# Alternating wide and narrow matmuls in the gate and up products of eight feed-forward stages

## The reference

```
def rms_norm(x, g):
    return x * rsqrt(mean(x * x) + eps) * g

def swiglu_ffn(h, w_gate, w_up, w_down):          # 1024 -> 2816 -> 1024
    return (silu(h @ w_gate) * (h @ w_up)) @ w_down

x = x + 0.5 * swiglu_ffn(rms_norm(x, g), w_gate, w_up, w_down)     # eight of these
```

## Time and profile before

| | |
|---|---|
| median of 3 runs | 2270.24 us (2267.35 to 2273.36) |
| the profiled execution: its own time | 2273.36 us |
| its span, first to last instruction | 2271.6 us |
| mean granted TensorE clock | 0.980 |
| TensorE matmuls busy | 2154.5 us (95%) |
| weight loads busy | 1839.9 us (81%) |
| VectorE / ScalarE / GpSimd busy | 1529.0 / 1147.1 / 355.5 us |
| DMA | 375.61 MB, 165 GB/s on average |

### The profile page before, as it was taken

One profiled execution on the slowest core, in us unless ns is written; L12 is line 12 of the kernel. 1 busy time (PEld: TensorE's weight loads), 2 busy tenths in 40 slices (PEclk: granted clock), 3 DMA queues, 4 the chain that ended last, 5 costly groups with the idle time before them and its releaser, 6 DMA issues.

```text
span 2271.6 us, 40266 instructions
## 1 busy us (share of the span) xinstructions
PE 2154.5 (95%) x14196; PEld 1839.9 (81%) x14196; DVE 1529.0 (67%) x2387; ACT 1147.1 (50%) x1945; POOL 355.5 (16%) x474
## 2 busy tenths in 40 slices
PE   7999899999999899989999999997999998879997
PEld 6888678888888688878888988886888688858885
DVE  5667956676668766666666756666666794667665
ACT  5446655455547554555455554446544642235544
POOL 1111111112111011111110001111111012311110
PEclk9999999999999999999999999998999999989998
DMA  6555435555555245545565446554655330115552
GB/s 236 195 186 183 135 103 200 191 171 177 193 194 181 87 154 191 192 156 195 186 222 188 152 161 203 186 189 180 208 191 169 132 127 18 50 65 198 188 188 97
DMA packets 103827, 375.61 MB, mean 165 GB/s; under 512 B 11536, under 2 KB 11920, under 8 KB 103728
## 3 DMA queue, kind: packets, MB, share of 16 engines
q1 hardware_dynamic: 103728, 374.24, 48.8%
HBM read 373.15 MB, written 1.05 MB: 165 GB/s over the span
## 4 chain that ended last, share of the span: by engine, by line
PE 84%; DVE 9%; ACT 4%; issue 2%; POOL 1%; DMA 0%; SPq 0%; DVEq 0%; ACTq 0%; POOLq 0%
PE bank L795 27%; PE bank L799 14%; PE bank L186 12%; PE bank L187 12%; PE bank L188 12%; DVE w_lo L180 3%; PE bank L1929 2%; DVE work L1293 1%; ACT w_hi L173 1%; ACT act L410 1%; PE bank L356 1%; ACT work L399 1%; DVE act L508 0%; DVE work L1317 0%; PE bank L1939 0%
## 5 line engine op out<-in xcount | busy, mean ns | idle before, releaser
L795 PE MATMUL bank<-act,w_hi 128*128 128x512 f32 x2816 | 709.3, 394 | 5.3 <-DVE act L508 5.3
L795 PEld LDWEIGHTS bank<-act,w_hi 128*128 128x128 f32 x2816 | 519.8, 190 | 109.2 <-DVE w_lo L180 4.7
L712 DVE TENSOR_TENSOR w_lo<-raw,w_hi 128x1024 fp32r<-128x1024 f32 x432 | 502.8, 1219 | 2.5
L703 ACT ACTIVATE w_hi<-raw 128x1024 fp32r<-128x1024 f32 x432 | 425.0, 1050 | 2.4
L799 PEld LDWEIGHTS bank<-act,w_lo 128*128 128x128 f32 x2816 | 385.1, 191 | 27.8
L799 PE MATMUL bank<-act,w_lo 128*128 128x256 f32 x2816 | 393.3, 283 | 0.0
L180 DVE TENSOR_TENSOR w_lo<-raw,w_hi 128x1024 fp32r<-128x1024 f32 x248 | 295.2, 1220 | 96.5 <-ACT w_hi L173 96.1
L765 DVE TENSOR_TENSOR work<-bank,work 128x256 f32<-128x256 f32 x176 | 74.7, 424 | 387.4 <-ACT work L727 387.4
L742 POOL TENSOR_TENSOR work<-work,rb 128x256 f32<-128x256 f32 x176 | 129.7, 737 | 1053.5 <-DVE work L762 1053.5
L173 ACT ACTIVATE w_hi<-raw 128x1024 fp32r<-128x1024 f32 x248 | 251.6, 1051 | 58.0 <-PE bank L188 57.8
L186 PE MATMUL bank<-w_hi,g_hi 128*128 128x512 f32 x704 | 277.1, 394 | 0.9 <-DVE w_lo L180 0.3
(11 more groups left out here) (270 smaller groups left out, 2280.4 us busy)
## 6 DMA issues: line engine op xcount, KB each, us to landing
raw<-w_dram SPq DMA_DIRECT2D x680, 512.0 KB, 4.4
work<-rows_dram SPq DMA_DIRECT2D x13, 512.0 KB, 6.0
work<-rrows_dram SPq DMA_DIRECT2D x5, 512.0 KB, 3.2
x<-x_dram SPq DMA_DIRECT2D x2, 512.0 KB, 3.8
out<-x SPq DMA_DIRECT2D x4, 256.0 KB, 2.1
work<-g_dram SPq DMA_DIRECT2D x1, 640.0 KB, 9.0
const<-const_dram SPq DMA_DIRECT2D x1, 512.0 KB, 6.0
work<-dist_dram SPq DMA_DIRECT2D x2, 256.0 KB, 5.2
```

The lines of the kernel that those rows point to most:

```text
L703: nc.scalar.activation(c.w_hi[:, n % RING, :], c.raw[:, n % RING, :], ACT.Copy).then_inc(c.hi_ready, 1)
L712: nc.vector.tensor_tensor(c.w_lo[:, n % RING, :], c.raw[:, n % RING, :], c.w_hi[:, n % RING, :].bitcast(F32), ALU.subtract).then_inc(c.lo_ ...
L795: nc.tensor.matmul(bank[:, :], c.w_hi[:, slot(m), k * P:(k + 1) * P], c.act[:, k, :, :], start=k == 0, stop=False)
```

## The change

`by_high` and `by_low` become one function that issues the wide and the narrow matmul of one k. `hidden` alternates them: wide, narrow, wide, narrow, over the eight k. The start of a stage gives up its two halves: for each k it waits for the tile and issues wide and narrow of the gate unit, then wide and narrow of the up unit. The instructions, their operands and their number stay the same, as does the last matmul of each unit.

```diff
-    def by_high(m, bank, k):
-        nc.tensor.matmul(bank[:, :], c.w_hi[:, slot(m), k * P:(k + 1) * P], c.act[:, k, :, :], start=k == 0, stop=False)
-    def by_low(m, bank, k):
-        return nc.tensor.matmul(bank[:, 0:S], c.w_lo[:, slot(m), k * P:(k + 1) * P], c.act_hi[:, k, :],
-                                start=False, stop=k == KT - 1)
+    def hidden_tile(m, bank, k):
+        w = slice(k * P, (k + 1) * P)
+        nc.tensor.matmul(bank[:, :], c.w_hi[:, slot(m), w], c.act[:, k, :, :], start=k == 0, stop=False)
+        return nc.tensor.matmul(bank[:, 0:S], c.w_lo[:, slot(m), w], c.act_hi[:, k, :], start=False, stop=k == KT - 1)
 
     def hidden(pe, i, m, bank):
         unit_waited(pe, i, m)
         for k in range(KT):
-            by_high(m, bank, k)
-        for k in range(KT):
-            last = by_low(m, bank, k)
+            last = hidden_tile(m, bank, k)
         last.then_inc(c.unit_used, 1)
...
     def tensor(pe):
         unit_waited(pe, None, 0)
         unit_waited(pe, None, 1)
-        for half in (range(4), range(4, KT)):
-            for k in half:
-                join.tile_there(pe, k)
-                by_high(0, gate[0], k)
-                by_high(1, up[0], k)
-            for m, bank in ((0, gate[0]), (1, up[0])):
-                for k in half:
-                    last = by_low(m, bank, k)
-                if k == KT - 1:
-                    last.then_inc(c.unit_used, 1)
+        for k in range(KT):
+            join.tile_there(pe, k)
+            gate_last = hidden_tile(0, gate[0], k)
+            if k == KT - 1:
+                gate_last.then_inc(c.unit_used, 1)
+            up_last = hidden_tile(1, up[0], k)
+        up_last.then_inc(c.unit_used, 1)
         join.spread_rows(pe)
         pe_step(pe, None, 1)
```

## The result

The changed kernel takes 2286.32 us (median of 4 runs, 2283.87 to 2287.91) against 2270.55 us for the kernel before in the same comparison: ratio 1.0068, 95% interval 1.0051 to 1.0087, or 11.6 to 19.8 us slower. The forecast was 2261.3 us, faster, with a range of 2245 to 2284. Both the direction and the range failed.

A forecast was written before the change was run, and what follows sets the result against it. TensorE's own matmul stream was taken as the bound. Savings of 8.8 us in the loop and 0.1 at the starts took 2273.36 us to 2264.5, or 2261.3 for the median; range 2245 to 2284.

The forecast's parts named there:

- What bounds the kernel: Inside feed-forward stages only TensorE's own stream binds; the wide and narrow matmuls make 41% of the path.
- Every narrow matmul now stands right behind a wide one and every wide one right behind a narrow one.: Loop after the change: narrow 114 ns, wide 232, together 346 a pair against 349.2; 8.8 us saved over 2760 pairs.
- the 27 ns that the down products pay: First five wide matmuls of L186 to L188, behind the up unit's narrow ones: some 27 ns extra per step.
- The 232 named as the upper bound: Wide matmul behind a narrow one in the loop: between 226.7 and 232 ns, with 232 taken.
- In a row of narrow ones it sets the pace at 120: Loading the next weights hides behind a wide matmul, but limits consecutive narrow ones to 120 ns each.
- The load behind each narrow matmul binds: Rival for the loop: the wide one's load takes 120 ns behind each narrow one; pair 352 ns, 2278 us; chance 0.22.
- Disturbed throughout: Rival for the loop: wide ones 232, narrow 117 to 119 ns; pair 349 to 351, 2270 to 2273 us; chance 0.22.
- Settles completely: Rival for the loop: only rows of several narrow matmuls disturb wide ones; pair 340 ns, 25 us gained, 2245; chance 0.17.
- The range's upper end: Slowest total time allowed: 2284 us, from a loop pair of 354 ns, above the 352 of the load rival.
- The 2760 pairs: Wide-narrow pairs counted at full clock: 2816 pairs scaled by the mean granted clock of 0.980.
- The rule weighed in the prediction: Skill formula, columns / 2.4 + 2.5 ns per matmul, loads hidden: a pair 325 ns before and after, zero gain.
- The starts: Stage starts taken tile by tile: L373 0.13 us sooner, 0.03 left behind L180; together worth 0.1 us.

The follow-up runs named there:

- e6: Against the kernel before: narrow matmuls of the gate unit alternate with wide ones of the up unit, so neighbours write different banks; step 8.340 us, one execution 2286.52 us.
- e13: Against the kernel before: loop alternates wide and narrow matmuls, the narrow widened to 512 columns, so both have equal width; step 9.973 us.

## Why the prediction was wrong

**What bounds the kernel: right.** TensorE's stream, without waits, before and after. No other engine, no DMA and no change of the granted clock in the repeated steps took part.

**The step that failed: "Every narrow matmul now stands right behind a wide one and every wide one right behind a narrow one. ... rows show each of the two transitions once per unit."** The prices themselves do occur: the first narrow one takes 113 ns and the wide one behind it 232 (233 behind a row of eight). But only every third pair has them. The second pair takes 117 and 241, the third 120 and 236, and then it begins again. The forecast had 114 and 232 for all; the means are 116.9 and 236.4. Those two terms make 7.3 of the 8.2 ns by which a pair was mis-sized (354.2 against 346). The rest is a term that the sum left out: the 27 ns that the down products pay were in the price of a pair now and not in the price after, and they are still paid. Over a step, 15 pairs of 353.3, one of 340 (the first wide, the last narrow) and the 27 give 5667 ns, or 354.2 a pair. The 232 named as the upper bound for a wide one behind a narrow one was no bound: it is the mean of the five in the earlier trace rows, and the second of those five is 236 by itself. None of the rows that the prediction read holds a lone narrow matmul between wide ones, so the price was carried over from another context.

**"In a row of narrow ones it sets the pace at 120": wrong.** The load was my explanation for 120 against 113. Rows of 320 columns, too long for that load to matter, pay the same 13.3 ns over their columns (147), and so do settled rows of 512 (226.7) and the end of a row of 384 (173). The 120 is the settled price and the 113 the exception. The 113 was measured as taken, but that it is half of 226.7 explains nothing: settled rows of 256 columns cost 120.

**The rivals.** "The load behind each narrow matmul binds" named 352 ns and 2278 us; the loop's cycle is 353.3 and the time 2286. The sum was near and the sign right by luck: its sign, 120 from L799 to L795, shows only in every third pair, and the 320 columns refute its reason. "Disturbed throughout" (349 to 351) had the mechanism that is nearest to what the starts show, a stream that never settles, priced too low. "Settles completely" did not happen. The range's upper end was drawn at a pair of 354, which is the pair that was measured (354.2), and yet the time fell outside: 5.0 x 2760 pairs give 13.8 us or 2284, and the comparison gave 11.6 to 19.8 slower. The 2760 pairs came from the mean clock of 0.980, but the lower clock falls mostly on waits: only 8 pairs ran at it. With 2808 the sums would move by 2%, which changes nothing.

**The rule weighed in the prediction.** By columns / 2.4 + 2.5 (the Trainium skill, TensorE: Matmul & The Clock Gate, section "Back-to-back issue gap") the order could not matter. The page states the formula for a single matmul by itself, and the prediction applied it to a stream. At the full clock no row shows that pace for these operands: 226.7 and 120 against 215.8 and 109. Every experiment with unlike widths disagrees with it. With 512 columns throughout, alternating costs nothing, as by the rule, but the level is 226.7.

**The starts: right.** Forecast 0.13 us gained at L373 and 0.03 left behind L180; measured 0.10 and 0.04 in stage 2, 0.09 and 0.05 in stage 4, and the kernel with that part alone can't be told from the kernel before.

**What stays open.** Why a matmul's overhead over its columns swings between some 7 ns (113 at 256 columns) and some 28 (241 at 512) where it settles at 13.3. It depends on the widths in sequence, not on the bank (e6) or on the change of weight tensor alone (e13), repeats from step to step, and is absent at the lower clock. What in TensorE's reading or loading falls in and out of step was not found; that the price comes from such a rhythm is inferred from the repeating patterns, not shown.

## What to carry to other kernels

A transition that a trace shows once between two long rows has a price in that context only; in a stream that consists of nothing but transitions it can cost more, and here it turned a forecast gain of 9 us into a loss of 15. When a change reorders a stream that is itself the bound, run one short variant of the order first, and read starts over many steps: 157.82 / 19 settles 10 ns where a single row settles none. And an order that shortens each step can still lose at the ends of a stage, where a result is needed sooner than in the loop.

## What the runs showed of the hardware

- In these kernels, at full clock, a settled stream of fp32r matmuls, each with its own load of 128 columns, costs columns / 2.4 + 13.3 ns: 120, 147 and 226.7 ns for 256, 320 and 512 columns. At the lower clock it costs columns / 1.2 and nothing more (213 and 427 ns).
- Alternating widths cost 33.3 ns a pair over the columns instead of 26.7, settled: cycle of 353.3 ns at 256 columns, and 33.3 for the whole step at 384. Two and two cost less (28.3) than four and four (32.1).
- The steps seem to come in whole multiples of 6.67 ns, 16 columns at 2.4 GHz: 1243, 1244, 1246, 1247, 1253, 1258, 1310, 1321, 1384, 1388 and 1496 times 6.667 give the eleven steps of the table to within half a nanosecond. If no change of width cost anything, a step with 256 columns would be 12 x 226.7 + 16 x 346.7 = 8267 ns, or 1240 of them. Above that, rows of sixteen pay 3, pairs 4, rows of eight 6, threes 7, fours 13 and alternating 18. The number of changes in a step is 2, 16, 4, 12, 8 and 32, so neither few nor many changes are cheap as such.
